# Three of the MLP's products moved into the end of the output projection, with the projection's buffers laid out anew

## What is computed

```python
y_x = mixer_out(h_x, kv_all, g_cq[l], w_uq[l], g_qn[l], w_conv[l], w_o[l], ropes)
x = layer_norm(ALPHA * x + mx[:, 2] * y_x, ln1_g[l], ln1_b[l])
y_x = sq_relu_mlp(x * (1.0 + mx[:, 4]) + mx[:, 3], w_mlp1[l], w_mlp2[l])
x = layer_norm(ALPHA * x + mx[:, 5] * y_x, ln2_g[l], ln2_b[l])
```

## Time and profile before

| | us |
|---|---|
| runs, median of 3 (lowest to highest) | 3060.58 (3053.29 to 3061.61) |
| the profiled execution's own time | 3056.14 |
| its span in the trace | 3054.3 |
| TensorE busy in it | 2930.5 |
| VectorE busy in it | 2275.4 |

### The profile page before, as it was taken

One profiled execution on the slowest core, in us unless ns is written; L12 is line 12 of the kernel. 1 busy time (PEld: TensorE's weight loads), 2 busy tenths in 40 slices (PEclk: granted clock), 3 DMA queues, 4 the chain that ended last, 5 costly groups with the idle time before them and its releaser, 6 DMA issues. The chain is left out here.

```text
span 3054.3 us, 43133 instructions
## 1 busy us (share of the span) xinstructions
PE 2930.5 (96%) x15760; PEld 2200.5 (72%) x15760; DVE 2275.4 (74%) x3182; ACT 1320.1 (43%) x1891; POOL 1382.7 (45%) x833
## 2 busy tenths in 40 slices
PE   5999978999999999999999979999999999999997
PEld 3889855566666566666658858887888888887786
DVE  4445456788887888888778887776777767887788
ACT  3222233444444444444443355555555543443342
POOL 1233324677767867686732243333333144214420
PEclk7999989999999999999999989999999999999999
DMA  6232379524354332434147875447444588787883
GB/s 261 60 88 78 102 229 327 122 73 82 97 119 95 84 78 62 89 75 84 38 141 263 288 293 190 153 153 299 152 152 152 199 317 290 286 312 286 296 296 138
DMA packets 252012, 526.64 MB, mean 172 GB/s; under 512 B 35568, under 2 KB 110832, under 8 KB 240624
## 3 DMA queue, kind: packets, MB, share of 16 engines
q1 hardware_dynamic: 245296, 498.33, 50.6%
q10 hardware_dynamic: 6528, 25.82, 2.1%
HBM read 363.19 MB, written 160.76 MB: 172 GB/s over the span
## 5 line engine op out<-in xcount | busy, mean ns | idle before, releaser
L1340 DVE TENSOR_REDUCE h_mpart<-a_mx 128x1 f32<-128x512 f32 x920 | 537.3, 631 | 154.1 <-PE a_mx L1445 140.7
L1269 POOL TENSOR_TENSOR a_acc_p<-a_acc_p,a_pf 128x1024 f32<-128x1024 f32 x237 | 572.8, 2417 | 152.0 <-ACT a_pf L1320 121.6
L1320 ACT ACTIVATE a_pf<-o_y 128x1024 f32<-128x1024 f32 x432 | 442.1, 1027 | 381.6 <-PE o_y L1492 374.6
L2513 PE MATMUL f_bank<-slots,f_wx 128*128 128x512 f32 x2304 | 534.3, 392 | 14.3 <-DMA slots<-s_uc 8.7
L2521 PE MATMUL f_bank<-slots 128*128 128x512 f32 x2352 | 538.9, 390 | 5.9 <-DVE slots L2292 5.9
L2521 PEld LDWEIGHTS f_bank<-slots 128*128 128x128 f32 x2352 | 442.1, 188 | 99.5 <-DVE slots L2292 7.6
L2513 PEld LDWEIGHTS f_bank<-slots,f_wx 128*128 128x128 f32 x2304 | 436.2, 190 | 107.3 <-DMA slots<-s_uc 10.3
L2459 POOL TENSOR_TENSOR f_work<-raw_rows 128x512 f32<-128x512 f32 x160 | 220.5, 1380 | 381.2 <-DVE f_wx L2285 369.3
L2468 POOL TENSOR_TENSOR f_y<-f_y,raw_rows 128x1024 f32<-128x1024 f32 x72 | 198.4, 2756 | 344.3 <-DMA raw_rows<-in_w 344.3
L2306 DVE TENSOR_TENSOR f_work<-f_work,f_bank 128x512 f32<-128x512 f32 x256 | 174.2, 680 | 135.1 <-ACT f_work L2184 124.3
L553 PE MATMUL p_main<-win_hi,u_hi 128*128 128x512 f32 (+2 forms) x528 | 196.7, 373 | 15.4 <-PEq L75 14.5
(11 more groups left out here) (280 smaller groups left out, 5062.1 us busy)
## 6 DMA issues: line engine op xcount, KB each, us to landing
raw_rows<-s_hx SPq DMA_DIRECT2D x112, 512.0 KB, 4.3
f_y<-in_w SPq DMA_DIRECT2D x104, 512.0 KB, 5.5
raw_rows<-in_w SPq DMA_DIRECT2D x72, 512.0 KB, 6.0
raw_rows<-in_w SPq DMA_DIRECT2D x32, 1024.0 KB, 4.9
s_hx<-stream SPq DMA_DIRECT2D x128, 256.0 KB, 2.7
s_hx<-f_work SPq DMA_DIRECT2D x96, 256.0 KB, 2.0
raw_rows<-in_w_ada SPq DMA_DIRECT2D x8, 2048.0 KB, 8.8
low<-s_mix SPq DMA_DIRECT2D x32, 512.0 KB, 5.4
```

The source lines that it names most:

```text
L1269: nc.gpsimd.tensor_tensor(acc[:, :], left[:, :], pf[(b * KT + kt) % NPF][:, :], ALU.add).then_inc(added_p, 1)
L1320: nc.scalar.activation(pf[n % NPF][:, :], sc[n % 2][:, :], ACT.Exp, scale=SCALES[0 if is_mla(b) else 1]).then_inc(exped, 1)
L1340: nc.vector.reduce_max(mpart[b % 2][:, s + 4 * half, k:k + 1], bank(("pair", c), half)[:, 0:CHUNKS[k][1]], AX.X).then_inc(mx_read, 1)
L2513: mm = nc.tensor.matmul(by_pair(bank[:, m % 8, :]), w[:, k], x[s][:, :, k * P:(k + 1) * P], start=(k == 0 and j == 0), stop=(k == 3 and j ...
```

## The change

Five things, none of which changes what is computed:

- The left factors of the first three positions are made in the projection, behind tile 7 (`left_sum`, `left_high`, `left_low`), and TensorE does these three products (`early_product`) around the last tile's turn: one before it, two after it. The last turn goes to `y[1]`, the products to two banks of their own and one of `y[0]`. The MLP begins with position 3 (`EARLY_LEFT`).
- Pair 6 is cut in two: positions 0 to 2 behind tile 14, positions 3 to 6 behind tile 15 (`BEHIND`); its last two sums go to the buffer of x, its last high and low part to a spare slot.
- The slots of positions 3 to 6 are loaded by ScalarE in the projection (`load_slots`), behind the last root.
- SP no longer waits for its last stores at the projection's end; the MLP's engines wait for them where they need them (`sums_stored`, and waits on `x1_stored`).
- To make room, the buffers are laid out anew, in one area that the MLP goes on using. x1 is made in place in the buffer of x; a load of x waits for the store of x1 two tiles before, and is asked for one tile ahead, behind the high parts.

The diff, cut to its core:

```diff
...
-        x, r, x1 = ([sb(f"{n}{i}", [P, D])[:, :] for i in range(2)] for n in ("x", "r", "x1"))
...
+        x = [wide(rows, 2 * i) for i in range(2)]
+        u, u_last = stream_tiles(g.u), stream_tiles(area[:, 0:4, :])
+        aside = g.slot_lo[SPARE]
...
+        LEFT_AT = 7
...
+        BEHIND = 3
...
-            for p in range(PAIRS + 1):
+            for p in range(PAIRS):
...
+            store_row(TT - 2)
+            store_sums(PAIRS - 1, range(0, BEHIND))
+            store_row(TT - 1)
+            store_sums(PAIRS - 1, range(BEHIND, NP))
             sp.wait_ge(cols_in, 16)
             sp.wait_ge(mlp_in, 32)
-            uses = ring_use(PAIRS - 1, NP - 1) + 1
-            for e in range(RING):
-                sp.wait_ge(uc_stored[e], 32 * ((uses - e + RING - 1) // RING))
-            for i in range(2):
-                sp.wait_ge(x1_stored[i], 16 * (TT // 2))
...
             def load_x(s):
                 t = TILE[s]
-                if s >= 2:
-                    act.wait_ge(y_read, s - 1)
+                need(act, x1_stored[s % 2], 16 * (s // 2))
                 act.dma_start(x[s % 2], a["x"][t * P:(t + 1) * P, :]).then_inc(x_in[s % 2], 16)
...
+            def load_slots():
+                act.wait_ge(y_done, TT)
+                for e in range(RING):
+                    act.wait_ge(uc_stored[e], 32 * ring_uses(ring_use(3, NP - 1) + 1, e))
+                for j in range(DIRECT, NP):
+                    for part, t in enumerate((g.slot_hi, g.slot_lo)):
+                        act.dma_start(raw(t[slot_of(j)]), g.uc[0, j, part]).then_inc(g.slot_in[slot_of(j)], 16)
...
             for s in range(TT):
-                if s:
+                if s and s < TT - 1:
                     stream(s - 1)
                 act.wait_ge(var_set, s + 1)
                 nc.scalar.activation(rstd[:, :], var[:, :], ACT.Sqrt, scale=-2.0).then_inc(std_set, 1)
-                if s + 2 < TT:
-                    load_x(s + 2)
                 if s and (s - 1) % 2:
-                    highs((s - 1) // 2)
+                    highs((s - 1) // 2, range(BEHIND) if s == TT - 2 else range(NP))
+                if 1 <= s < TT - 1:
+                    load_x(s + 1)
+                if s == LEFT_AT:
+                    for pos in range(EARLY_LEFT):
+                        left_high(pos)
+            load_slots()
+            highs(PAIRS - 1, range(BEHIND, NP))
+            stream(TT - 2)
             stream(TT - 1)
...
-                if s >= 2:
-                    dve.wait_ge(x1_stored[s % 2], 16 * (s // 2))
-                nc.vector.tensor_tensor(x1[s % 2], at, ln_g, ALU.mult).then_inc(scaled, 1)
+                nc.vector.tensor_tensor(x[s % 2], at, ln_g, ALU.mult).then_inc(scaled, 1)
                 dve.wait_ge(scaled, s + 1)
-                nc.vector.tensor_tensor(x1[s % 2], x1[s % 2], ln_b, ALU.add).then_inc(x1_set, 1)
+                nc.vector.tensor_tensor(x[s % 2], x[s % 2], ln_b, ALU.add).then_inc(x1_set, 1)
...
             for s in range(TT):
                 work(s)
                 if s and (s - 1) % 2:
-                    lows((s - 1) // 2)
+                    lows((s - 1) // 2, range(BEHIND) if s == TT - 2 else range(NP))
+                if s == LEFT_AT:
+                    for pos in range(EARLY_LEFT):
+                        left_low(pos)
+            lows(PAIRS - 1, range(BEHIND, NP))
...
+            def early_product(pos):
+                pe.wait_ge(g.left_lo_set, pos + 1)
+                pe.wait_ge(lo_set, NP * 4)
+                if pos == 2:
+                    pe.wait_ge(y_read, TT - 1)
+                first_product(nc, g, early_bank[pos], left_hi[pos], left_lo[pos], pos).then_inc(g.m_done, 1)
+            early_product(0)
             turn(TT - 1)
+            early_product(1)
+            early_product(2)
...
-            for j in range(DIRECT, NP):
-                uc_load(sp, j)
...
-            for pos in range(NP):
+            for pos in range(EARLY_LEFT, NP):
                 high(0, pos)
+            sums_stored(act)
...
```

More of the change, by code:

```diff
@@ L1610, in right_parts, with stream_tiles, left_parts, first_product @@
     return quarter[first], quarter.get(second), sign
-def stream_tiles(g):
-    return [g.u[:, 2 * i:2 * i + 2, :].rearrange("p c (k t) -> p (c k) t", t=P) for i in range(2)]
+def stream_tiles(t):
+    return [t[:, 2 * i:2 * i + 2, :].rearrange("p c (k t) -> p (c k) t", t=P) for i in range(2)]
+EARLY_LEFT = 3
+FIRST_BANK = 6
+SPARE = (NP + 4) % SLOTS
+WX_AT = 12
+def left_parts(raw, n, key):
+    k, f = {"11": (0, 0), "12": (4, 0), "21": (0, P), "22": (4, P)}[key]
+    return raw[:, n % 2, k:k + 4, f:f + P]
+def first_product(nc, g, out, left, left_lo, pos):
+    s = slot_of(pos)
+    left, left_lo = (t.rearrange("p (k f) -> p k f", k=4) for t in (left, left_lo))
+    for k in range(4):
+        for j, (w, x) in enumerate(((left, g.slot_hi), (left, g.slot_lo), (left_lo, g.slot_hi))):
+            mm = nc.tensor.matmul(by_pair(out), w[:, k], x[s][:, :, k * P:(k + 1) * P], start=(k == 0 and j == 0), stop=(k == 3 and j == 2))
+    return mm
 def by_pair(t):
@@ L1642, in stage_mix @@
         y = g.y
-        t_x = ps("t_x", [P, 2, 512])
+        t_x, early = (g.banks.enter_context(nc.psum_tensor("o_" + n, [P, 2, 512], F32)) for n in ("t_x", "early"))
+        g.eight = [t[:, half, :] for t in (y[0], y[1], t_x, early) for half in range(2)]
+        early_bank = [early[:, 0, :], early[:, 1, :], y[0][:, 0, :]]
         rows_in, cols_in, cols_set = sem("rows_in"), sem("cols_in"), sem("cols_set")
@@ L1673, in target_free, with total_of @@
             use = ring_use(p, pos)
-            if use is not None:
+            if (p, pos) == LAST_SUM:
+                eng.wait_ge(y_done, TT)
+            elif use is not None:
                 need(eng, uc_stored[use % RING], 32 * (use // RING))
         sums_before = lambda p, pos: len(SUMS["right"]) * p + SUMS["right"].index(pos)
+        sum_aside = lambda p, pos: p == PAIRS - 1 and pos >= NP - 2
+        def total_of(p, pos):
+            return by_tile(rows[:, pos - NP + 2, :]) if sum_aside(p, pos) else total[sums_before(p, pos) % SUM_RING]
+        ring_uses = lambda end, e: sum(1 for use in range(end) if use % RING == e)
+        g.uc_all = [32 * ring_uses(ring_use(PAIRS - 1, NP - 1) + 1, e) for e in range(RING)]
         summed_lows = lambda k: NP * (k // len(SUMS["right"])) + SUMS["right"][k % len(SUMS["right"])] + 1
@@ L1833, in _ @@
                     sums((s - 1) // 2)
+                if s == LEFT_AT:
+                    for pos in SUMS["left"]:
+                        if pos < EARLY_LEFT:
+                            left_sum(pos)
         @block.tensor
@@ L1877, in stage_mlp @@
         hx = {pos: unit(11 + k) for k, pos in enumerate(SUMS["left"])}
-        tail_u = stream_tiles(g)
+        tail_u = stream_tiles(work[:, 0:4, :])
         tail_total = unit(11)
-        spare = (NP + 4) % SLOTS
-        tail_hi, tail_lo = ([unit(7 + 2 * pos + part).bitcast(F32R) if pos < 2 else t[spare][:, (pos - 2) % 4, :] for pos in range(NP)]
+        tail_hi, tail_lo = ([unit(7 + 2 * pos + part).bitcast(F32R) if pos < 2 else t[SPARE][:, (pos - 2) % 4, :] for pos in range(NP)]
                             for part, t in enumerate((slot_hi, slot_lo)))
@@ L2485, in _ @@
             for pos in SUMS["left"]:
-                sums(0, pos)
+                if pos >= EARLY_LEFT:
+                    sums(0, pos)
+            sums_stored(pool)
             for n in range(PAIRS):
@@ L2497, in _ @@
                 hf, q = divmod(n, NQ)
-                for pos in range(NP):
+                for pos in range(0 if n else EARLY_LEFT, NP):
                     m = NP * n + pos
```

139 lines of the change are left out of this document (97 added, 42 removed).

## The result

The change makes the kernel slower: 3094.19 us in the median (3090.48 to 3096.96) against 3060.58 before, ratio 1.0118 [1.0098, 1.0137]. The range ended at 3089. The profiled execution took 3094.19 us, its span 3092.4, 38.1 more than before.

What follows compares the result with a forecast made beforehand. TensorE, busy 96% of the span, was taken to bound the kernel, with VectorE just in time. Projection loss 26.6 us less seam gain 11.1 is 15.5 on 3056.1: 3071.6, named as 3073; range 3059 to 3089.

Steps and rivals of the forecast that it cites:

- the likeliest case: The forecast itself: odd tiles wait for x in the projection, the seam gains less than that, 3073 us; chance 0.55.
- rival C: Seam: last stores collide with slot loads, gain falls to 5 us, 3078 (3083 with odd loads of 6.0); chance 0.15.
- I take 5.2: Projection, odd tiles 3 to 13: x's load takes 5.2 us, each tile starts 3.9 late, 23.2 in all.
- the bound of 28: Projection: upper bound on the six odd tiles' loss, 28 us, with loads of 6.0 us issued 1.34 before need.
- Rival A: Projection: x's loads find a quiet moment and land in 3.6 us, odd tiles lose 13.6, total 3061; chance 0.22.
- No cover: Projection: VectorE's 4 us of rest per pair lie inside the low parts and shift, so they hide no load delay.
- Even tiles 1 us, the left factors 2.4: Projection: tiles 4, 6, 10, 12, 14 lose 1 us together; left factors cut at tile 7 cost VectorE 2.4 us.
- The fourth product 12.0 earlier: Seam: the MLP's fourth product begins at 1792.1 where it began at 1804.07, 12.0 us earlier.
- Later waits: MLP's start: ScalarE and GpSimd wait for the last stores behind their first factors; cost nothing, covered by 11 us of products.
- 2.8 of slow clock: Seam: TensorE rests about 7 us, so 2.8 us of slow clock come back in the fourth product.
- The wait of 1.95 for the last slot goes: Seam: slot loads issued 15 us earlier land by 1799.6, needed at 1803.1, so TensorE's 1.95 us wait disappears.
- 22.1 us: no more is to be had at the seam: Seam: TensorE's waits and slow-clock losses in the kernel before add to 22.1 us, the most the change could win there.

Runs made afterwards that it cites:

- mix tile later: Changed kernel, but SyncE asks for a pair's second mix tile behind the sums' stores: 3066.27 us, ratio 1.0038 to the kernel before.
- loads moved back: Changed kernel, but at even steps x's load stands ahead of the high parts again: 3048.31 us, ratio 0.9991 to the kernel before.
- second half in the MLP: Changed kernel, x loaded early, slots 3 and 4 asked early, 5 and 6 as SyncE's first MLP work: 3047.46 us, ratio 0.9974 to before.
- slots in halves: Changed kernel, x loaded early, ScalarE asks early for slots 3 and 4, SyncE for 5 and 6 behind the last stores: 3048.51 us, ratio 0.9982 to before.
- slots thin: Changed kernel, x loaded early, only 64 KB of each 1 MB slot load for positions 5 and 6: 3041.90 us, ratio 0.9965 to before.
- slots last: Changed kernel, x loaded early, slot loads behind ScalarE's last two streams: 3055.58 us, ratio 1.0015 to the kernel before.

## Why the prediction was wrong

**The direction was right, and so was the reason**: the odd tiles wait for x, and TensorE with them. It was the likeliest case that came, with the mechanism of rival C on top.

- *"I take 5.2" for an odd load* failed in its size. From issue to use the six took 6.6 to 7.2 us, 6.86 on average, each then 5.4 late in place of 3.9: 32.6 us for the 23.2 of the sum, and over the bound of 28 too. The five rows it was taken from the earlier trace rows were loads asked for two tiles ahead, in other company: right behind the mix tile, as the moved load is, but with none of the sums' stores. The issues around the one of 6.0, from 1709 to 1713 of the kernel before:

```profile
low<-s_mix SPq DMA_DIRECT2D x2, 512.0 KB, 4.9
...
o_x<-in_x ACTq DMA_DIRECT2D x1, 512.0 KB, 6.0
```

At the new place two or three stores of 256 KB each are asked for between the mix tile and the load. That is 0.5 to 0.75 MB, an estimated 1.2 to 1.9 us at 422 GB/s; the six loads land 6.8 us after their issue on average, 1.6 more than 5.2. The 2.4 us that the run with the mix tile later took out are thus not what the sum lacked: the five rows had them too. Rival A names the stores, but no term of the sum prices them. No run moved them alone, so this part is read from the issues and not tested. The bounds were taken from the load's own rows when the load had been put into other traffic.

- *No cover* held: the loss up to the first low part of pair 6 is 36.8 us, of which 32.6 are these waits.
- *Even tiles 1 us, the left factors 2.4* were about right: tiles 4 to 14 waited for no x, and VectorE took up tile 8 5.05 us after norming tile 7, where 3.25 is usual: 1.8.
- *The fourth product 12.0 earlier* was right at 13.15; the clock fell in the rest before it, as said.
- *"Later waits ... I cost this at nothing; its cover is those products, 11 us"* failed. The wait was 12.2 us on ScalarE, because the last stores took 20.3 us to land. TensorE waited 2.50 us for the left factor that ScalarE's wait made late, and lost clock with it. Step 0 to step 1 took 29.9 us for 23.1, the next step 20.7 for 19.0: 8.4 lost, where 0.85 (2.8 of slow clock less 1.95 for the slot) had been reckoned. The seam gave 13.15 - 8.4 = 4.7 us in place of 11.1.
- *"The wait of 1.95 for the last slot goes"* failed with it. The last slot was used 27.25 us after the first was asked for (1818.16 to 1845.41), where the loads had needed 23.2 by themselves: the stores were among them, and TensorE waited 2.95.
- *"22.1 us: no more is to be had at the seam"* left out a clock loss. Behind the wait of 1.95 the next 48 matmuls took 1827.16 - 1814.55 = 12.61 us, where 48 at the later pace take 10.88. It doesn't enter the sum.
- *Rival C* named this: stores and loads collide, ScalarE waits for the stores, the seam falls to 5. Its chance of 0.15 was too low for something whose premises stood in the rows: 2.5 MB of stores and 8 MB of loads at a DMA share of 1.0. Its sum, 3083, took odd loads of 6.0.

The sum with the terms put right: 32.6 + 1.8 + 0 - 4.7 = 29.7 on 3056.1, and with the 2.4 us of the 36.8 that no term names, 3088.2. The 6 us from there to the profiled 3094.2 lie outside the changed stretch (4.8 ahead and 1.2 behind it); the 4.8 are scatter, for that first matmul comes at 1574.72 in the trace with the loads moved back and at 1580.17 in the one with the second half in the MLP, which have the same instructions up to there. On the median, the 32.1 us up to step 2's landmark give 3060.58 + 32.1 = 3092.7 of the 3094.19 measured.

The Trainium skill (DMA: Bandwidth & Descriptors, Issuing engines are not separate DMA queues) holds that DMAs of all issuing engines interleave on the same 16 DMA engines. By that rule, the trace agrees: the last stores on SyncE's queue took 20.3 us while ScalarE's 8 MB came in, and a load on ScalarE's queue was 2.4 us shorter once SyncE's 1 MB was out of its way.

## What to carry to other kernels

Price a moved transfer by what is in flight at its new place, bytes at the measured rate ahead of it, on whichever engine's queue, not by the duration it had where it stood. When a wait for stores is moved later and loads are asked for earlier, check whether they fall into the same full stretch: the loads' early start then holds back the very stores that the moved wait is for. Ask first for what is needed first, then let the stores go, then the rest; by the ratios the run here that does so is some 5 us of 3054 faster than the one that only moves x's loads back, with intervals that overlap.

## What was not expected of the hardware

The last stores of 256 KB took 20.3 us to land beside eight loads of 1 MB, though these stood on another engine's queue. The issues of the projection's last stores (count, KB each, median us to landing), in the kernel before, where no slot is under way:

```profile
s_uc<-o_ring_hi SPq DMA_DIRECT2D x2, 256.0 KB, 2.5
s_uc<-o_ring_lo SPq DMA_DIRECT2D x2, 256.0 KB, 3.0
```

With the slots in halves, 4 MB of slots asked for 6.6 to 8.0 us ahead and 4 MB behind:

```profile
s_uc<-slots SPq DMA_DIRECT2D x2, 256.0 KB, 12.1
```

And with the slots thin, 4.25 MB ahead and none behind:

```profile
s_uc<-slots SPq DMA_DIRECT2D x2, 256.0 KB, 11.9
```

So 2.5 to 3.0 us without slots, 11.9 to 12.1 with 4 MB ahead, 20.3 with 8 MB. The second 4 MB cost 8.2 us when asked for ahead of the stores, and at 422 GB/s they take 9.9; asked for behind the stores they cost them next to nothing (12.1 for 11.9).

I had expected a transfer of 256 KB to get its share of the engines at once. The landings in the traces show that it got a turn instead. In the run with the slots last, stores and loads are asked for side by side from 1784.5 on, and they land by turns: a load of 1 MB every 3.1 us from 1792.67 to 1811.25, seven of them, and 0.5 to 0.6 us behind each a store of 256 KB. So a store waited as long as the load beside it, and a row of stores as long as a row of as many loads. The changed kernel's 20.3 us came about in the same way. Seven other stores (one of them x1's row) stood ahead of the last pair on its own queue; five of them landed one between each two loads, from 1829.66 to 1845.37, and the other two and the last pair within 2.7 us of the last load. What the engines count, transfers or rows (a load and a store are both 128 rows, of 8 KB and 2 KB), was not tried.
